# Three weight splits and one activation split change places in the VectorE and ScalarE programs of a two-layer hybrid trunk

## The reference

```python
h = x
# layer 0
qkv = rmsnorm(h) @ w_qkv + b_qkv               # 16 query heads, 2 key/value heads of 64
q, k = partial_rope(q), partial_rope(k)        # first 16 of 64 elements rotated
p = exp(s - m); p = p / (sum(p) + exp(sink - m))   # chunks of 64, window 128
h = h + (p @ v) @ w_o
h = h + (silu(g) * u) @ w_down                 # dense SwiGLU, d_ff 3584
# layer 1
z, xbc, dt = split(rmsnorm(h) @ w_in)
xs, B, C = split(silu(causal_conv4(xbc)))      # SSD scan over 8 groups of 4 heads
h = h + rmsnorm((scan(xs, dt, B, C) + d * xs) * silu(z)) @ w_out
logits = rmsnorm(h) @ w_router                 # top 2 of 8 experts
h = h + sum_e combine[e] * swiglu(rmsnorm(h), w_gu[e], w_down[e])
out = rmsnorm(h)
```

## Time and profile before

| | |
|---|---|
| runs, median (lowest to highest) | 1601.34 us (1601.16 to 1609.09) |
| the profiled execution's own time | 1601.24 us |
| its span, first to last instruction | 1599.5 us |
| TensorE (PE) busy | 1541.1 us, 96% |
| VectorE (DVE) busy | 1235.1 us, 77% |
| ScalarE (ACT) busy | 1023.6 us, 64% |
| mean granted TensorE clock | 0.977 |

### The profile page before, as it was taken

One profiled execution on the slowest core, in us unless ns is written; L12 is line 12 of the kernel. 1 busy time (PEld: TensorE's weight loads), 2 busy tenths in 40 slices (PEclk: granted clock), 3 DMA queues, 4 the chain that ended last, 5 costly groups with the idle time before them and its releaser, 6 DMA issues.

```text
span 1599.5 us, 21555 instructions
## 1 busy us (share of the span) xinstructions
PE 1541.1 (96%) x7791; PEld 1301.6 (81%) x7791; DVE 1235.1 (77%) x1069; ACT 1023.6 (64%) x943; POOL 60.9 (4%) x97
## 2 busy tenths in 40 slices
PE   7899999999999897999999999999999999999997
PEld 6788888888999875788888888888888888888885
DVE  6555555455798755898898898898898898898996
ACT  5455444346577543777877877777777776777774
POOL 2015000000000000100000000000000000000020
PEclk9799999999999898999999999999999999999999
DMA  9149855545443232999999999999999999999997
GB/s 340 57 140 396 327 179 184 203 157 161 132 133 106 106 123 76 375 383 380 386 380 377 384 383 368 394 378 377 385 386 376 385 375 383 378 380 385 414 387 293
DMA packets 166233, 476.25 MB, mean 298 GB/s; under 512 B 9153, under 2 KB 35025, under 8 KB 166177
## 3 DMA queue, kind: packets, MB, share of 16 engines
q1 hardware_dynamic: 157152, 446.73, 75.3%
q0 software_dynamic: 5888, 19.23, 3.1%
q10 hardware_dynamic: 3136, 9.54, 1.5%
HBM read 454.49 MB, written 20.97 MB: 297 GB/s over the span
## 4 chain that ended last, share of the span: by engine, by line
PE 85%; DVE 6%; DMA 3%; ACT 2%; issue 2%; DVEq 1%; SPq 0%; ACTq 0%
PE bank L745 26%; PE bank L747 26%; PE bank L746 26%; DMA ring<-moe_w_gu_in 2%; DVE w_lo L1290 2%; DVE acc L1581 1%; PE bank L1173 1%; DMA ring<-swa_w_qkv_in 1%; ACT w_hi L434 1%; DVE arg L1605 1%; PE bank L855 1%; DVE w_lo L1651 1%; PE bank L1091 1%; PE bank L764 0%; PE bank L1160 0%
## 5 line engine op out<-in xcount | busy, mean ns | idle before, releaser
L1651 DVE TENSOR_TENSOR w_lo<-ring,w_hi 128x2048 fp32r<-128x2048 f32 x336 | 763.5, 2289 | 84.8 <-PE bank L747 74.1
L641 ACT ACTIVATE w_hi<-ring 128x2048 fp32r<-128x2048 f32 x336 | 636.3, 1920 | 150.4 <-DMA ring<-moe_w_gu_in 95.1
L745 PE MATMUL bank<-w_hi,xgT_hi 128*128 128x512 f32 x896 | 351.6, 392 | 3.4 <-DVE w_lo L1651 2.3
L747 PE MATMUL bank<-w_hi,xgT_lo 128*128 128x512 f32 x896 | 349.7, 390 | 0.0
L746 PE MATMUL bank<-w_lo,xgT_hi 128*128 128x512 f32 x896 | 349.3, 390 | 0.0
L1290 DVE TENSOR_TENSOR w_lo<-ring,w_hi 128x2048 fp32r<-128x2048 f32 (+1 forms) x84 | 190.0, 2265 | 121.2 <-ACT w_hi L434 120.6
L434 ACT ACTIVATE w_hi<-ring 128x2048 fp32r<-128x2048 f32 (+1 forms) x84 | 159.0, 1898 | 122.2 <-PE bank L747 115.4
L745 PEld LDWEIGHTS bank<-w_hi,xgT_hi 128*128 128x128 f32 x896 | 168.7, 188 | 38.3 <-DVE w_lo L1651 2.7
L747 PEld LDWEIGHTS bank<-w_hi,xgT_lo 128*128 128x128 f32 x896 | 168.6, 188 | 35.4
L746 PEld LDWEIGHTS bank<-w_lo,xgT_hi 128*128 128x128 f32 x896 | 168.6, 188 | 34.3
L745 PE MATMUL bank<-w_hi,m_hT_hi 128*128 128x512 f32 x448 | 175.8, 392 | 0.0
(11 more groups left out here) (299 smaller groups left out, 1710.2 us busy)
## 6 DMA issues: line engine op xcount, KB each, us to landing
ring<-moe_w_gu_in SPq DMA_DIRECT2D x230, 1024.0 KB, 7.1
ring<-moe_w_down_in SPq DMA_DIRECT2D x112, 1024.0 KB, 7.3
ring<-ffn_w_gu_in SPq DMA_DIRECT2D x28, 1024.0 KB, 6.8
ring<-ffn_w_down_in SPq DMA_DIRECT2D x14, 1024.0 KB, 4.8
xg_rows<-zeros POOLq DMA_DIRECT2D x36, 256.0 KB, 12.3
ring<-ssm_w_in_in SPq DMA_DIRECT2D x8, 1024.0 KB, 5.0
ring<-ssm_w_in_in SPq DMA_DIRECT2D x16, 512.0 KB, 3.8
ring<-ssm_w_in_in SPq DMA_DIRECT2D x32, 256.0 KB, 4.3
```

The lines of the kernel that those rows point to most:

```text
L641: act.activation(w_hi[:, c % HI], ring[:, c % RING], ACT.Copy).then_inc(hi_ready, 1)
L745: pe.matmul(o, stat[0], mov[0], start=start, stop=False)
L747: return pe.matmul(o, stat[1], mov[0], start=False, stop=stop)
L1651: dve.tensor_tensor(w_lo[:, c % SPLIT], ring[:, c % RING], w_hi[:, c % HI].bitcast(F32), ALU.subtract).then_inc(lo_ready, 1)
```

## The change

Four edits, all in the order of the two programs; nothing is added or removed.

- Attention, VectorE: the split of chunk 5 (`ahead(5)`) moves from ahead of the first rotation to behind the copies of the transposed vectors.
- Attention, VectorE: the split of chunk 7 (`ahead(7)`) moves from ahead of the division of the first eight heads (`normed(0, 0)`, `normed(0, 1)`) to behind it.
- SSD loop, both engines: the y split of group s - 3 now stands ahead of the split of chunk GR0 + 2s + 4.
- Routing, both engines: the split of expert chunk 1 moves behind the residual of tile 0 on VectorE, and behind the first two copies of h's transposes on ScalarE. Chunk 0 stays.

```diff
--- before.py
+++ after.py
@@ -614,8 +614,6 @@
                         ins = act.activation(arg[:, 2, r], bank[5][:, r * P:(r + 1) * P], ACT.Exp,
                                              bias=acol[:, 2 * SH + g * REP + r:2 * SH + g * REP + r + 1])
                     ins.then_inc(c_exp, 1)
-                if s < G:
-                    ahead(GR0 + 2 * s + 4)
                 g = s - 3
                 if g >= 0:
                     act.wait_ge(c_yT, g + 1)
@@ -625,6 +623,8 @@
                     for k in range(2):
                         act.activation(yT_hi[:, 2 * g + k], bank[7][:, k * T:(k + 1) * T], ACT.Copy,
                                        scale=vT[:, 32 + 2 * g + k:33 + 2 * g + k]).then_inc(c_yThi, 1)
+                if s < G:
+                    ahead(GR0 + 2 * s + 4)
             ahead(MOE0 - 1)
             act.wait_ge(c_conv, G)
             act.wait_ge(c_sq, 2 * G)
@@ -641,10 +641,12 @@
                     act.activation(w_hi[:, c % HI], ring[:, c % RING], ACT.Copy).then_inc(hi_ready, 1)
 
 
-            ahead_e(0, 0, 2, SPLIT)
+            ahead_e(0, 0, 1, SPLIT)
 
             load_roots(3)
             for i in range(4):
+                if i == 2:
+                    ahead_e(0, 1, 2, SPLIT)
                 act.wait_ge(xT_mm, 12 + i + 1)
                 part = (slice(None), slice((i % 2) * 4, (i % 2) * 4 + 4), slice((i // 2) * P, (i // 2 + 1) * P))
                 act.activation(hT[part], bank[4 + i][:].rearrange("p (a b) -> p a b", b=P), ACT.Copy).then_inc(raw_T, 1)
@@ -1358,8 +1360,6 @@
             dve.drain()
             dve.tensor_scalar(trig[:, 2], trig[:, 2], -3.1415925, 3.1415925, ALU.max, ALU.min).then_inc(angle_done, 1)
 
-            ahead(5)
-
             def rope(head, n):
 
                 v = qkv[:, :, head * HD:(head + n) * HD].rearrange("p t (h d) -> p t h d", d=HD)
@@ -1390,6 +1390,7 @@
             dve.wait_ge(vec_T, 1)
             dve.tensor_copy(vT[:, 16:80], bank[7][:, 0:64])
             dve.tensor_copy(cwT[:].rearrange("p a b -> p (a b)"), bank[7][:, P:2 * P]).then_inc(vec_sb, 1)
+            ahead(5)
             dve.wait_ge(bc_loaded, 5 * 16)
             dve.tensor_scalar(sinks[:].rearrange("p (b a) -> p b a", b=2),
                               sinks_in[:].rearrange("p (a b) -> p b a", b=2), -1.0, None, ALU.mult)
@@ -1440,9 +1441,9 @@
             biased(1, 512, 512, bank[5][:], bias_q1)
             dve.drain()
             rope(HEADS // 2, HEADS // 2).then_inc(rope_done, 1)
-            ahead(7)
             normed(0, 0)
             normed(0, 1)
+            ahead(7)
             largest(1, 0)
             largest(1, 1)
             ahead(8)
@@ -1651,8 +1652,10 @@
                     dve.tensor_tensor(w_lo[:, c % SPLIT], ring[:, c % RING], w_hi[:, c % HI].bitcast(F32),
                                       ALU.subtract).then_inc(lo_ready, 1)
 
-            ahead_e(0, 0, 2)
+            ahead_e(0, 0, 1)
             for t in range(TT):
+                if t == 1:
+                    ahead_e(0, 1, 2)
                 dve.wait_ge(*((so_first, 1), (chunk_used, SO0 + KI // 2))[t])
                 for n in range(2):
                     hh = h[:, t, 512 * n:512 * (n + 1)]
```

## The result

The changed kernel takes 1585.49 us in the median of four runs (1583.43 to 1587.71), beside 1603.37 us (1601.16 to 1609.09, four runs) for the kernel before. Its median was 1601.34 when the forecast was made; a fourth run of 1605.40 us moved it. The ratio is 0.9886 with a 95% interval of 0.9859 to 0.9914: 1.1% faster. The profiled execution took 1585.58 us (span 1583.8), 15.7 us less than the one of before. Run again beside other kernels, the changed kernel gave 1584.24 us and a ratio of 0.9884 (0.9859 to 0.9908).

A forecast was written before the change was run, and what follows sets the result against it. TensorE, 85% of the chain that ended last, was taken as the bound, so only its idle or half-clock time could be regained. 5.7 + 2.2 + 5.8 + 4.0 = 17.7 us off 1601.24 gave 1583.5 us, range 1576 to 1590.

The forecast's parts named there:

- First edit: Attention, chunk 5's split behind the vector copies: first scores start at 41.1 instead of 46.82, 5.7 us sooner.
- new wait for chunk 5: Attention: TensorE, no longer held by the rotations, waits some 1.5 us for the split of chunk 5.
- Second edit: Attention, chunk 7's split behind the division: the division moves forward by the whole split, TensorE restarts 2.2 us earlier.
- first rival: Attention stays at full clock with one wait left: 5 us more gained, 1578.5 us; chance 0.33.
- Third edit: SSD loop, y split ahead of the weight split: two long rounds shrink by 2.9 us each, 5.8 us.
- VectorE's and ScalarE's round takes over: SSD loop: the bound changes hands, convolutions come 18.7 us apart, TensorE's own round being 17.7.
- Fourth edit: Routing, expert chunk 1's split behind the first residual: 5.8 us sooner, less 1.8 for half clock, 4.0 us.
- first load of the expert loop: End of the routing, SP's queue: this load was to start 17 us sooner than 631.07.
- fourth rival: SSD loop: weight splits wait for the y transposes and delay convolutions by 20.5 us, 1609.8 us; chance 0.04.

The follow-up runs named there:

- fill_wait: The changed kernel with nine matmuls whose results nobody reads in TensorE's wait for the second rotation in attention: 1582.96 us, ratio 0.9872.
- pad_after: The changed kernel with three idle maxima on VectorE in four steps of the SSD loop: 1589.09 us, one run.
- high_half_earlier: The changed kernel with ScalarE's high half of the loop's moved chunk put into its idle time ahead of the exponentials: 1581.48 us, ratio 0.9856.
- rot_only: The kernel before with only the split of chunk 5 moved behind the copies of the transposed vectors: 1599.33 us, ratio 0.9970.
- div_only: The kernel before with only the split of chunk 7 moved behind the division: 1601.41 us, ratio 0.9982.
- chunk1_later: The changed kernel with expert chunk 1's split behind both residuals on VectorE and all four copies on ScalarE: 1582.17 us, ratio 0.9859.
- route_only: The kernel before with only expert chunk 1's split moved, behind tile 0's residual and ScalarE's first two copies: 1599.10 us, ratio 0.9969.
- pad_before: The kernel before with three idle maxima on VectorE in four steps of the SSD loop: 1610.47 us, one run.
- changed_again: The changed kernel run once more, unaltered, beside the version with three further edits: 1583.35 to 1587.54 us.

## Why the prediction was right

The forecast was 1583.5 us within 1576 to 1590; the first comparison gave 1585.49, a later one 1584.24. By its own steps, all from the profiled executions, in which 15.7 us were gained for 17.7 forecast:

- **First edit, 5.7 us.** The scores start 46.82 - 41.53 = 5.3 us sooner. The new wait for chunk 5 came as worked out (1.5 forecast, 1.40 measured), and the clock stayed up over it. Of the missing 0.4 us, 0.3 was there before the edit: TensorE stopped that much later, since its first matmuls ran slow for longer in this execution (to 15.9 us for 14.6). Only 3.2 of the 5.3 us are the shorter wait. The rest is half clock in the kernel before, from 40.19 on, which the forecast took over with the 46.82 without saying so:

```profile
38.60:45.30 6.70, 5.11 (x18) 0.50 0.28 70
```

  This part varies: the scores start at 45.34 to 46.82 us in the five traces without the edit and at 41.16 to 42.04 in the eight with it.
- **Second edit, 2.2 us.** The transposes of the weights start 60.66 - 53.15 = 7.5 us sooner, 2.2 more than the scores. Exact. The remaining wait stayed 2.38 us and attention went slow, the forecast and not the first rival. The rival was priced at 5 us: with full clock throughout (`fill_wait`) the product did start 5.4 sooner, but a slow stretch behind it took 1.7 back.
- **Third edit, 5.8 us.** The last convolution comes 537.56 - 524.04 = 13.5 us sooner, 5.8 more than the 7.7 of attention. The step that carried this, that two waits of 4.7 us and two slow stretches are not worth their sum because VectorE's and ScalarE's round takes over, held to a tenth, and `pad_after` and `high_half_earlier` show it from both sides. That there were two slow stretches to remove was a property of the execution that was read: the loops of `rot_only` and `div_only` had one, and their three rounds take 60.7 and 59.1 us for 62.0. The 18.7 us were already to be read in the kernel before, in the one round in which VectorE did not wait for TensorE.
- **Fourth edit, 4.0 us.** TensorE takes up the second tile's transposes at 600.70 for 618.48, 17.8 us sooner. Between the loop and there 1.7 us had been lost: of the 13.5, the y transposes of the last step but one kept 11.8, chiefly to a slow stretch from 555 us on. So the edit moved them by 6.0 us, as worked out (5.8). The clock took 2.7 of it, and not 1.8: 0.9 on the transposes and 1.8 on the router matmuls. Net 3.3 for 4.0. `chunk1_later` shows that it was the 3.4 us wait that brought the clock down.
- **Carried to the end.** The router's last matmul comes 15.1 us sooner, and so does the first load of the expert loop (616.01 for 631.07; the forecast said 17); the end of the span comes 15.7 sooner. Nothing of substance is gained or lost among the experts, as the full stretch of the earlier trace rows said.

The differences from the forecast are therefore -0.4 (first edit), +0.2 (the rest of attention), -1.7 (between the loop and the routing), -0.7 (fourth edit) and +0.6 (to the end), together -2.0 us: the mechanisms held, and no large errors had to cancel. The chain of waits gave the places; the sum of its waits would have given a wrong size. What the forecast had no means to size is where the slow stretches fall and how long they last. The runs of one kernel spread over up to 10.5 us (the kernel before), as much as two of the edits together. On this the Trainium skill ("TensorE: Matmul & The Clock Gate", section "What's actually happening") says that the moment of a change is not tied to the program: the pair of 1.9 us waits above agrees, 1.91 us at full clock behind it and 1.89 us at half.

The fourth rival, that the loop's weight splits come late, had no part in it: on ScalarE the high half waited for nothing, and the split ended before U was there in each step.

## What to carry to other kernels

Where a wait repeats in a loop, look for the rounds in which it is absent: their length is what the other engines can do, and the gain from removing the wait is the difference of the rounds, not the wait. Then read the clock behind it, and in more than one execution. On an engine whose program holds work for later and work that another engine waits for now, put the latter first, and then read which wait is last in its place. A wait of TensorE can cost more by the half clock behind it than by itself (here nothing at full clock and 2.9 us at half, for the same 1.9 us), so it is best left where little work follows, or filled.

## What the runs showed of the hardware that was not expected

- The same wait of 1.9 us in the same place was followed by half clock in two executions (the kernel before, `route_only`) and by full clock in two others (`rot_only`, `div_only`), and the loop's round was 21.6 or 18.7 us by that alone.
- The length of the slow stretch did not follow the wait ahead of it: 6.8 and 10.2 us behind the same 2.81 us (`div_only`, `rot_only`), 10.2 behind 2.60, 3.5 and 4.4 us (`pad_after`, `pad_before`). TensorE was busy all through the 10.2 us of `rot_only` without getting its full clock back.
- The clock also fell with no wait just ahead: at 44.9 us in `changed_again`, after 6.05 us in which TensorE was busy throughout, the last 3.1 of them with the small matmuls of the scores.
- Matmuls that nobody needs made a kernel's stage faster: 2.2 us of them brought the output product to 65.5 us (two traces) from 68.0 to 72.3 (five traces), while the kernel's median fell by 1.3 to 2.5 us, which is within the noise.
